# Even attention of a two-model chain: a loop over pairs of heads, with scores issued alternately in two row halves

## The reference

```
keys, values = 256 tokens of context, then the 512 tokens      # 768 keys
scores = q[hd] @ keys.T                                        # 512 x 768
p      = exp(scores - max(scores, axis=-1))
out    = (p @ values) / p.sum(axis=-1)
```

## Time and profile before

| | us |
|---|---|
| median of three runs | 3258.86 |
| the three runs | 3260.21, 3258.86, 3250.52 |
| span of the profiled execution | 3258.9 |
| PE busy in it | 2947.2 (90%) |
| DVE busy | 1062.4 (33%) |
| ACT busy | 913.0 (28%) |

### The profile page before, as it was taken

The page is one execution under the profiler, slowest core; times in us unless marked ns, Lnnn a source line. Parts: engine busy times, 40 slices in busy tenths (PEclk is TensorE's granted clock), DMA queues, the critical chain, the costliest instruction groups (busy, mean ns, idle before and its releaser), DMA issues.

```text
span 3258.9 us, 41546 instructions
## 1 busy us (share of the span) xinstructions
PE 2947.2 (90%) x18407; PEld 2024.4 (62%) x18407; DVE 1062.4 (33%) x1573; ACT 913.0 (28%) x1498; POOL 0.2 (0%) x4
## 2 busy tenths in 40 slices
PE   6997899999998799999989998889898887999897
PEld 3765768888776677888767766654443454444443
DVE  3445642233545653224243244420010135000002
ACT  3443242232444333223243354221110032110011
POOL 0000000000000000000000000000000000000000
PEclk9998999999999899999989999989999998999999
DMA  7224323323223422322263105479999953999997
GB/s 273 78 104 156 105 65 95 99 88 97 78 90 113 156 71 78 101 93 91 94 217 124 39 1 207 142 291 410 409 407 408 406 210 117 388 409 409 403 408 291
DMA packets 251539, 637.28 MB, mean 196 GB/s; under 512 B 12896, under 2 KB 110176, under 8 KB 251232
## 3 DMA queue, kind: packets, MB, share of 16 engines
q1 hardware_dynamic: 248224, 627.22, 51.9%
q10 hardware_dynamic: 3136, 7.40, 0.6%
HBM read 632.48 MB, written 2.10 MB: 195 GB/s over the span
## 4 chain that ended last, share of the span: by engine, by line
PE 70%; DMA 12%; DVE 7%; ACT 5%; PEld 2%; issue 2%; PEldq 1%; SPq 1%; ACTq 0%; DVEq 0%
PE ps L641 67%; DMA ring<-in_w_exp_up 6%; DMA ring<-in_w_exp_gate 5%; PE ps L655 3%; PEld ps L641 2%; ACT h L1653 1%; ACT mix_halves L1656 1%; PEldq L1112 1%; DMA ring<-in_ada_w 1%; SPq L629 0%; DVE work L2394 0%; DVE work L3038 0%; DMA ring<-in_w_mod 0%; DVE small L2952 0%; DVE work L2954 0%
## 5 line engine op out<-in xcount | busy, mean ns | idle before, releaser
L641 PE MATMUL ps<-mix_halves,work_halves 128*128 128x512 f32 (+1 forms) x1544 | 622.5, 403 | 44.7 <-DVE h_halves L2245 34.4
L641 PE MATMUL ps<-h_halves,work_halves 128*128 128x512 f32 (+1 forms) x1544 | 609.7, 395 | 6.2 <-DVE mix_halves L2245 3.9
L641 PE MATMUL ps<-mix_halves,ring_halves 128*128 128x512 f32 x1448 | 569.1, 393 | 0.0
L641 PE MATMUL ps<-ring,work 128*64 128x512 f32 x1552 | 395.5, 595 | 57.5 <-DMA ring<-in_w_exp_up 31.6
L2245 DVE TENSOR_TENSOR ring_halves<-ring,work_halves 128x2048 fp32r<-128x2048 f32 (+2 forms) x125 | 252.6, 2021 | 551.9 <-ACT work_halves L1576 453.5
L641 PEld LDWEIGHTS ps<-mix_halves,work_halves 128*128 128x128 f32 (+1 forms) x1544 | 291.1, 189 | 131.9 <-issue 49.2
L641 PEld LDWEIGHTS ps<-h_halves,work_halves 128*128 128x128 f32 (+1 forms) x1544 | 291.9, 189 | 73.8 <-issue 6.4
L641 PEld LDWEIGHTS ps<-mix_halves,ring_halves 128*128 128x128 f32 x1448 | 273.0, 189 | 60.8
L641 PEld LDWEIGHTS ps<-ring,work 128*64 128x64 f32 x1552 | 129.5, 137 | 270.7 <-issue 269.2
L1576 ACT ACTIVATE work_halves<-ring 128x2048 fp32r<-128x2048 f32 x102 | 188.2, 1845 | 336.7 <-PE ps L641 336.1
L641 PE MATMUL ps<-ring,proj 128*64 128x512 f32 (+1 forms) x1136 | 231.2, 546 | 3.1 <-issue 3.0
(11 more groups left out here) (396 smaller groups left out, 3405.7 us busy)
## 6 DMA issues: line engine op xcount, KB each, us to landing
ring<-in_w_exp_down SPq DMA_DIRECT2D x110, 1024.0 KB, 16.3
ring<-in_w_exp_gate SPq DMA_DIRECT2D x106, 1024.0 KB, 11.0
ring<-in_w_exp_up SPq DMA_DIRECT2D x88, 1024.0 KB, 15.2
ring<-in_ada_w SPq DMA_DIRECT2D x48, 1024.0 KB, 7.4
ring<-in_w_mod SPq DMA_DIRECT2D x48, 1024.0 KB, 7.5
ring<-in_w_in SPq DMA_DIRECT2D x22, 1024.0 KB, 5.3
ring<-in_w_gate SPq DMA_DIRECT2D x22, 1024.0 KB, 5.3
ring<-in_w_up SPq DMA_DIRECT2D x22, 1024.0 KB, 5.3
```

The lines of the kernel that those rows point to most:

```text
L641: i = pe.matmul(o, lhsT, rhs, start=start, stop=stop, **kw)
```

## The change

On all three engines the loop goes over the 16 pairs.

TensorE: `scores(pair)` issues the 512 keys of both heads, then the 256 keys of both, so that consecutive matmul calls alternate between the row halves. The loop waits for both exponentials of pair p, issues the scores of pair p+1, the output of pair p-1, the transposes of tile 2p, waits for `e_out`, and issues the transposes of tile 2p+1. ScalarE does both exponentials of pair p+1, then both copies of pair p. VectorE waits for both tiles' transposes of pair p-1, does both maxima of pair p+1, then copies the output of pair p-1. `e_prob` gets four buffers in place of two, since exponentials of pair p+1 are written before the transposes of pair p have been read; `e_probT` moves behind it in `work` and keeps two.

```diff
-        e_prob, e_probT = cut(work, 0, 1536, i=2, k=768), cut(work, 1536, 1536, i=2, j=6, q=P)
+        e_prob, e_probT = cut(work, 0, 3072, i=4, k=768), cut(work, 3072, 1536, i=2, j=6, q=P)
...
-                def scores(i):
-                    hd, n = unit(i)
-                    r = slice(hd % 2 * 64, hd % 2 * 64 + 64)
+                def scores(pair):
                     for b, (lo, hi) in enumerate(((0, 512), (512, 768))):
-                        mm(ps[:, i % 2 * 2 + b, 0:hi - lo], proj[r, hd // 2, n * P:n * P + P],
-                           e_krep[r, hd // 4, lo:hi], True, True, "score" if b else None)
+                        for s in range(2):
+                            hd, n = unit(2 * pair + s)
+                            r = slice(s * 64, s * 64 + 64)
+                            mm(ps[:, 2 * s + b, 0:hi - lo], proj[r, hd // 2, n * P:n * P + P],
+                               e_krep[r, hd // 4, lo:hi], True, True, "score" if b else None)
...
-                tiles = 8 * NT
+                pairs = 4 * NT
                 scores(0)
-                scores(1)
-                for i in range(tiles):
-                    pe.wait_ge(*due("pexp"))
-                    if i < tiles - 2:
-                        scores(i + 2)
-                    if i and i % 2 == 0:
-                        output(i // 2 - 1)
-                    if i > 2 and i % 2:
-                        pe.wait_ge(*due("e_out", 2 if i == 27 else 1))
-                    if i == tiles - 1:
+                for p in range(pairs):
+                    pe.wait_ge(*due("pexp", 2))
+                    if p < pairs - 1:
+                        scores(p + 1)
+                    if p:
+                        output(p - 1)
+                    if p == pairs - 1:
                         recip_rows((0, 1))
-                    turns(i)
-                output(tiles // 2 - 1)
+                    turns(2 * p)
+                    if p:
+                        pe.wait_ge(*due("e_out", 2 if p == 13 else 1))
+                    turns(2 * p + 1)
+                output(pairs - 1)
...
-                exponentials(0)
-                for i in range(8 * NT):
-                    if i < 8 * NT - 1:
-                        exponentials(i + 1)
-                    act.wait_ge(*due("probT"))
-                    bank = 4 + i % 2 * 2
-                    f(e_probT[:, i % 2, 0:4, :], ps[:, bank, :].rearrange("p (j q) -> p j q", j=4), ACT.Copy)
+                for s in range(2):
+                    exponentials(s)
+                for p in range(4 * NT):
+                    if p < 4 * NT - 1:
+                        for s in range(2):
+                            exponentials(2 * p + 2 + s)
+                    for s in range(2):
+                        act.wait_ge(*due("probT"))
+                        bank = 4 + s * 2
+                        f(e_probT[:, s, 0:4, :], ps[:, bank, :].rearrange("p (j q) -> p j q", j=4), ACT.Copy)
...
-                maxima(0)
-                for i in range(tiles):
-                    if i < tiles - 1:
-                        if i >= 1:
-                            dve.wait_ge(*due("probT"))
-                        maxima(i + 1)
-                    if i and i % 2 == 0:
-                        outputs(i // 2 - 1)
-                    if i == 25:
+                for i in range(2):
+                    maxima(i)
+                for p in range(tiles // 2):
+                    if p < tiles // 2 - 1:
+                        if p:
+                            dve.wait_ge(*due("probT", 2))
+                        for s in range(2):
+                            maxima(2 * p + 2 + s)
+                    if p:
+                        outputs(p - 1)
+                    if p == 12:
                         dve.wait_ge(*due("pexp", 24))
                         reciprocals(0, 24)
```

More of the change, by code:

```diff
@@ L1205, in turns @@
                     for j in range(6):
-                        turn(ps[:, bank + j // 4, j % 4 * P:j % 4 * P + P], e_prob[:, i % 2, j * P:j * P + P],
+                        turn(ps[:, bank + j // 4, j % 4 * P:j % 4 * P + P], e_prob[:, i % 4, j * P:j * P + P],
                              "probT" if j == 5 else None)
@@ L1990, in exponentials @@
                     s = ps[:, i % 2 * 2:i % 2 * 2 + 2, :].rearrange("p b k -> p (b k)")[:, 0:768]
-                    to("pexp", f(e_prob[:, i % 2, :], s, ACT.Exp, bias=stats[:, o + 1:o + 2], accum_out=e_den[:, i:i + 1]))
-                exponentials(0)
-                for i in range(8 * NT):
-                    if i < 8 * NT - 1:
-                        exponentials(i + 1)
-                    act.wait_ge(*due("probT"))
-                    bank = 4 + i % 2 * 2
-                    f(e_probT[:, i % 2, 0:4, :], ps[:, bank, :].rearrange("p (j q) -> p j q", j=4), ACT.Copy)
-                    to("probT_sb", f(e_probT[:, i % 2, 4:6, :], ps[:, bank + 1, 0:256].rearrange("p (j q) -> p j q", j=2),
-                                     ACT.Copy))
+                    to("pexp", f(e_prob[:, i % 4, :], s, ACT.Exp, bias=stats[:, o + 1:o + 2], accum_out=e_den[:, i:i + 1]))
+                for s in range(2):
[8 more added lines that the diff above has]
+                        f(e_probT[:, s, 0:4, :], ps[:, bank, :].rearrange("p (j q) -> p j q", j=4), ACT.Copy)
+                        to("probT_sb", f(e_probT[:, s, 4:6, :], ps[:, bank + 1, 0:256].rearrange("p (j q) -> p j q", j=2),
+                                         ACT.Copy))
             def mlstm():
@@ L2711, in attention @@
                     link(tt(mix[:, b, :], mix[:, b, :], ps[:, b, :], ALU.mult))
-                due("probT", 2)
+                due("probT", 4)
             def lower_block(s):
```

## The result

The changed kernel takes 3237.91 us (median of 5 runs, 3234.11 to 3247.16), the kernel before 3256.36 us (5 runs, 3250.52 to 3260.21). The ratio is 0.9947 with a 95% interval of 0.9931 to 0.9963: faster by 18.5 us, where 15.5 us were forecast, and by more than the 0.3% that can be told from no change.

The account below looks back on a forecast made before the run. TensorE was taken to set the pace of the even attention; side-by-side scores, a 5.02 us period, the slow beginning and the end summed to 15.5 us saved. 3258.9 - 15.5 = 3243.4 us, range 3235 to 3253.

Parts of the forecast that it names:

- Part 1: Even attention: scores of both heads run side by side in the row halves, removing 1.48 us of PE per pair.
- Part 2: Steady attention pairs: a loop through VectorE and ScalarE becomes the bound; period 5.02 us, saving 1.06 per pair.
- Loop C: Steady pair, T0 being its scores' start: both maxima, VectorE's output copy, second transposes; longest, T0 + 5.02 us.
- loop A: Steady pair: scores, two maxima, exponential, next scores, which could start 4.91 us after the pair's scores started.
- Loop B: Steady pair: ScalarE's two copies, 1.74 us together, delay the output; output and transposes end at T0 + 4.07.
- The 4.60 for PE's own work: Steady pair: period if only PE counted, 6.08 - 1.48 = 4.60 us; the lower bound of the period.
- Part 3: Stage's beginning, half clock until 1862.5 us: pair 2's scores start at 1855.7, pair 3's at 1863.5.
- Part 4: Twelve periods of 5.02 us and the stage's end: last output starts at 1936.4 instead of 1951.91, 15.5 us saved.
- One of the prediction's own signs of being wrong: Attention stage: the forecast is wrong if the granted clock between 1865 and 1935 us is below 1.00.
- the rival that they would absorb the gain: Experts' weight loads, 2200 to 2640 us: starting at their old time, they leave no gain, 3258.9 us; chance 4%.
- no data in this stage: Even attention: SyncE's queue moves no data (DMA share 0.00) because its buffers are full, so it costs nothing.
- The slow rival: Attention stage: PE's short standstills keep the clock at 0.50, period 8.48 us, 32 us slower, 3291 us; chance 4%.

Follow-up runs that it names:

- the version with the heads kept apart: Changed kernel with a tiny matmul over all 128 rows between the two heads' scores; 3261.75 us, ratio 1.0011 to the kernel before.
- the negated keys: Changed kernel plus the late wait, with replicated keys stored negated so that VectorE's negation goes away; 3241.31 us in a single run.
- the copy between the maxima: Changed kernel with VectorE's copy of the output moved in between the two maxima; 3242.81 us in a single run.
- the late wait: Changed kernel, but TensorE waits for VectorE's output copy only before the fifth of the second tile's six transposes; 3246.31 us in a single run.

## Why the prediction was right, point by point

Forecast were 3243.4 us, in a range of 3235 to 3253; measured were 3237.91, inside the range and 5.5 us below the forecast. Of these, 2.5 us are the base: the forecast started from 3258.9, the kernel before has a median of 3256.36 over five runs. The other 3.0 us are gain (18.5 against 15.5).

*Part 1, the overlap.* Right in mechanism and size: eight matmuls in 1.56 us, and with the overlap alone taken away the ratio to the kernel before is 1.0011.

*Part 2, the next bound.* Right that not PE but a loop through VectorE and ScalarE sets the period, and nearly right in size: 4.94 against 5.02. The step that failed is the choice among the three. Loop C was called the longest, at 5.02; the runs show loop A, forecast at 4.91. In loop C the copy was put behind the negation's end and a handoff, at T0 + 3.88. In the trace it starts 0.08 us before the negation ends (1888.57 against 1888.65), at T0 + 3.78, and the second transposes at T0 + 4.11, not 4.22. C so ends with A at 4.94 at the latest. A measured 0.03 above its forecast, and with C's wait moved away the period stayed at 4.94. Over twelve periods of 4.94 in place of 5.02 this is 1.0 us more gain. Loop B was overpriced as well: the two tiles' copies take 1.62 us (1884.64 to 1886.26), not 1.74, and the first starts while the accumulator is still being read, so that the output follows the scores after 1.52 us, not 1.80; the 0.3 us of standstill forecast before the output did not come. The 4.60 for PE's own work was too high as well: it kept 0.80 + 0.85 for the transposes, and twelve in a row take 1.46.

*Part 3, the beginning.* This is the term that was mis-sized. The stretch at low clock was kept at its old length, up to 1862.5. It was 3.41 us and not 13.65. From the first scores to those of pair 3 the forecast was 18.8 us (1844.75 to 1863.5), measured 15.1 (1840.02 to 1855.16): 3.6 us more gain. The effect was foreseen in the range (1.5 to 3 us), but not in the sum. No row in the prediction could have given the new length, and the old one was not fixed either: it was 10.24 us in the second profile of the kernel before, whose stage is 105.5 us, 1.6 us shorter. Against that profile the stage gains 17.1 us and not 18.7, so part of the extra gain is the luck of which execution was profiled.

*Part 4, the end.* From pair 15's scores to the last output 12.7 us were forecast and 14.0 measured (1914.42 to 1928.44). The order of the work was right. The last output but one came on time (6.6 us behind pair 15's scores, 6.7 forecast). A low stretch of the clock fell on the last output but one, 2.55 us from start to start in place of 1.47, and on the 32 matmuls behind it: 1.3 us less gain.

*The sum for the stage.* 15.5 + 1.0 + 3.6 - 1.3 = 18.8 us, measured 18.7. The misses are larger than their sum tells, since they partly cancel. One of the prediction's own signs of being wrong did appear: the granted clock between 1865 and 1935 was not at 1.00 throughout but 0.98 on average, because of the low stretch at the end. It cost 1.3 us, not the gain.

*The tail behind it.* The shift reached the end, as said. From the last output to the end of the span 1304 us pass in the changed kernel, 1307 in both profiles of the kernel before, and 1304 to 1312 in all ten. The experts' stretch, taken in the kernel before as far behind the last output as in the changed kernel:

```profile
2149.00:2624.00 475.00, 440.83 (x2306) 210.80 (x2307) 42.67 (x60) 52.81 (x100) 0.00 (x0) 1.00 1.00 395
```

The changed kernel has a DMA share of 1.00 and 396 GB/s there (above), so that the loads started earlier together with the stage; the rival that they would absorb the gain falls. The prediction's "no data in this stage" holds from 1862 on; before that its own row has a share of 0.10, which changes nothing in the sum.

*The slow rival.* PE does stand still for 0.26 us in each pair, and the clock stayed at 1.00 in the 64 us from 1850 to 1914. The rival falls. What the page "TensorE: Matmul & The Clock Gate" of the Trainium skill says in its section on psum-queue depth-cycling, that short idle moments between groups of matmuls make the clock go back and forth, did not happen in this steady part.

## What to carry to other kernels

Two sets of matmuls in different row halves shared the time of one here (1.56 us for the pair), as long as they stood next to each other in TensorE's stream; a tiny matmul over all rows between them took that away (3.11 us). When such a change takes TensorE off the critical path, draw each loop that returns to the freed place (scores, maximum, exponential, scores) from measured starts, not from durations: the forecast had three loops within 0.15 us of one another, and a copy that started 0.10 us earlier than forecast was enough to make another one bind. Then look for the smallest instruction on the binding loop: a negation of 0.15 us, hardly visible by its busy time, was worth 5.4 us. And when no wait is listed any more, check the distance from start to start against a place where nothing binds: 1.60 us against 1.46 showed that the loop was still there.

## What was not expected of the hardware

The low stretch of TensorE's clock at the stage's beginning was 13.65, 10.24 and 10.24 us in the three profiles with one head's scores at a time, and 3.41 or 6.83 us in all seven with both heads side by side. PE stood still before it in all of them, for 2.3 us in the kernel before and 3.35 in the changed kernel. The loop over pairs is not the cause, since the version with the heads kept apart has that loop and a stretch of 10.24. Short stretches go with heads side by side in all ten profiles. No run takes this apart from what comes with it, such as the longer standstill before it (2.99 to 3.35 us against 2.3), so the cause stays open.

At the end of the stage TensorE waits for the last pair but one's copies. In six profiles it did so for 1.56 to 2.63 us, and in four of these (1.56 three times, 2.00 once) a low stretch of 3.41 us followed; after 1.68 us with the negated keys and 2.63 us with the copy between the maxima there was none. In the four others, where the wait was 1.05 to 1.16 us or was filled, none came either. Such a wait may bring a low stretch and may not; its length alone doesn't tell.

Between executions the first scores of the stage stood anywhere from 1836.12 to 1847.64 us, though the work ahead of them is the same in all ten profiles but for the sign in one copy of the keys. This is as large as most effects studied here. A single run's time says little beside it (3246.31 for the late wait), while the stage's own length repeated to 0.1 us between two executions of the changed kernel.

ScalarE starts a copy before the one ahead has ended, in the kernel before too (1876.19 against 1876.30). In the changed kernel the four copies of 0.59, 0.38, 0.61 and 0.40 us, 1.98 in sum, are through in 1.62 (from 1884.64 on).
